# The entry of a gated-delta mixer on one core: unit order, gate rows and norm sums moved, one convolution placed in the delta rule

## The reference

```
qkv = silu(causal_depthwise_conv(h @ w_in[q, k, v], conv_w))        # 4 taps, 8 heads of 128
q, k = l2norm(q), l2norm(k)
beta = sigmoid(h @ w_in[b]);  g = -exp(a_log) * softplus(h @ w_in[a] + dt_bias)
o_a = gated_delta_rule_chunked(q, k, v, cumsum of g in chunks of 64, beta)
o_a = rmsnorm(o_a, dn_out_norm) * silu(h @ w_in[z])
o_b = stick_breaking_attention(rmsnorm(sb_q), rmsnorm(sb_k), sb_v)
x   = x + (sigmoid(ga) * (o_a @ w_branch_a) + sigmoid(gb) * (o_b @ w_branch_b)) @ w_out
```

## Time and profile before

| | us |
|---|---|
| median of 3 runs (lowest, highest) | 2456.24 (2454.42, 2457.91) |
| profiled execution | 2458.99 |
| its span, first to last instruction | 2457.2 |
| GpSimd busy | 1706.3 |
| VectorE busy, ScalarE busy | 1124.6, 1115.8 |
| first layer's mixer: unit 3 begins, last Gram product begins | 223.62, 266.74 |
| second layer's mixer: the same | 1056.27, 1099.40 |

### The profile page before, as it was taken

One profiled execution on the slowest core, in us unless ns is written; L12 is line 12 of the kernel. 1 busy time (PEld: TensorE's weight loads), 2 busy tenths in 40 slices (PEclk: granted clock), 3 DMA queues, 4 the chain that ended last, 5 costly groups with the idle time before them and its releaser, 6 DMA issues.

```text
span 2457.2 us, 40321 instructions
## 1 busy us (share of the span) xinstructions
PE 2352.2 (96%) x15688; PEld 2139.3 (87%) x15688; DVE 1124.6 (46%) x1945; ACT 1115.8 (45%) x1275; POOL 1706.3 (69%) x1340
## 2 busy tenths in 40 slices
PE   8999899999999999999999999999999999999997
PEld 7888889998988888888899889889888888888886
DVE  3335765422333333365554232333625665523766
ACT  4335344446443443454443544335555335555433
POOL 6998454554799899774455478997545997645995
PEclk9999999999999999999999999999999999999999
DMA  6555323323455555542333345565333555323553
GB/s 236 191 193 164 103 87 103 103 89 119 160 193 192 175 189 190 177 146 86 94 107 110 103 136 169 192 204 150 102 104 120 192 196 170 119 87 117 188 191 111
DMA packets 312197, 359.96 MB, mean 146 GB/s; under 512 B 18636, under 2 KB 291072, under 8 KB 311936
## 3 DMA queue, kind: packets, MB, share of 16 engines
q1 hardware_dynamic: 311866, 358.01, 44.8%
q10 hardware_dynamic: 198, 0.06, 0.0%
HBM read 357.00 MB, written 1.05 MB: 146 GB/s over the span
## 4 chain that ended last, share of the span: by engine, by line
PE 83%; DVE 10%; ACT 5%; issue 2%; POOL 1%; DMA 0%; ACTq 0%; DVEq 0%
PE ps L545 20%; PE ps L745 20%; PE ps L577 16%; PE ps L582 9%; PE ps L624 3%; PE ps L831 1%; PE ps L784 1%; PE ps L640 1%; PE ps L838 1%; PE ps L1116 1%; DVE sb_vT L1843 1%; DVE sb_kT L1843 1%; PE ps L840 1%; PE ps L611 1%; DVE sb_levels L1911 1%
## 5 line engine op out<-in xcount | busy, mean ns | idle before, releaser
L518 POOL TENSOR_TENSOR sb_lo<-sb_raw,sb_hi 128x512 fp32r<-128x512 f32 (+1 forms) x1336 | 1706.1, 1312 | 728.2 <-ACT sb_hi L1213 727.7
L1213 ACT ACTIVATE sb_hi<-sb_raw 128x2048 fp32r<-128x2048 f32 (+3 forms) x341 | 639.3, 1876 | 668.3 <-PE ps L582 349.2
L577 PE MATMUL ps<-sb_hT,sb_hi 128*128 128x512 f32 x1792 | 426.1, 390 | 0.0
L577 PEld LDWEIGHTS ps<-sb_hT,sb_hi 128*128 128x128 f32 x1792 | 332.7, 188 | 66.7
L745 PE MATMUL ps<-sb_hT,sb_hi 128*128 128x256 f32 x2304 | 312.4, 288 | 8.9 <-ACT sb_zT L1313 3.9
L745 PEld LDWEIGHTS ps<-sb_hT,sb_hi 128*128 128x128 f32 x2304 | 286.4, 191 | 15.3 <-ACT sb_zT L1313 4.3
L582 PEld LDWEIGHTS ps<-sb_hT,sb_lo 128*128 128x128 f32 x1792 | 229.8, 191 | 8.7
L582 PE MATMUL ps<-sb_hT,sb_lo 128*128 128x256 f32 x1792 | 232.4, 283 | 0.0
L1763 DVE TENSOR_TENSOR sb_yinv<-ps,sb_row 128x512 f32<-128x512 f32 x112 | 77.5, 692 | 334.9 <-PE ps L582 334.9
L545 PE MATMUL ps<-sb_hi,sb_o_h 128*128 128x512 f32 x560 | 219.5, 392 | 3.9 <-DVE sb_o_l L2219 3.0
L545 PE MATMUL ps<-sb_hi,sb_o_l 128*128 128x512 f32 x560 | 218.6, 390 | 0.0
(11 more groups left out here) (373 smaller groups left out, 3682.1 us busy)
## 6 DMA issues: line engine op xcount, KB each, us to landing
sb_raw<-in_ffn_w_in SPq DMA_DIRECT2D x88, 1024.0 KB, 5.1
sb_raw<-in_w_in SPq DMA_DIRECT2D x78, 1024.0 KB, 5.2
sb_raw<-in_ffn_w_out SPq DMA_DIRECT2D x44, 1024.0 KB, 4.9
sb_raw<-in_ffn_w_up SPq DMA_DIRECT2D x44, 1024.0 KB, 5.1
sb_raw<-in_ffn_w_down SPq DMA_DIRECT2D x22, 1024.0 KB, 4.8
sb_raw<-in_w_out SPq DMA_DIRECT2D x16, 1024.0 KB, 5.1
sb_raw<-in_w_branch_a SPq DMA_DIRECT2D x8, 1024.0 KB, 5.4
sb_raw<-in_w_branch_b SPq DMA_DIRECT2D x8, 1024.0 KB, 5.1
```

Source lines behind the costliest of these rows:

```text
L518: ins = nc.gpsimd.tensor_tensor(lo[:, slot, c], raw[:, slot, c], hi[:, slot, c].bitcast(F32), ALU.subtract)
L577: mm(ps[:, bank + i, :].rearrange("p (h n) -> p h n", h=2), wh[:, c, i * P:(i + 1) * P], hT_both[:, :, c, :], start=c == 0, stop=False, sk ...
L1213: fn(hi[:, slot, 0:width], raw[:, slot, 0:width], ACT.Copy).then_inc(hi_ready, 1)
```

## The change

Units 3 to 7 come in the order b, k, a, v, z. On TensorE the norm sums `pre(l, 0)` stand behind the second quarter of z, the small transposes of the gate rows between z and the last unit q1, and the 20 transposes are gone. ScalarE applies SiLU to q and k alone ahead of the squares (new helper `silus`) and to v and z behind the inverse roots; TensorE waits for the latter (`first_silu`) ahead of the transposes of k and v in the first delta rule. VectorE's gate rows use bank 7 instead of the bank of a, which is released as soon as a is read. VectorE no longer convolves q1 ahead of the first normalisation: it does so in two halves in the first delta rule, behind its first two steps, ahead of k1's halves. The plan and all later units are unchanged.

```diff
-FIRST = [("sv", 0), ("sv", 1), ("q", 0), ("z", 0), ("b", 0), ("k", 0), ("a", 0), ("v", 0), ("q", 1)]
+FIRST = [("sv", 0), ("sv", 1), ("q", 0), ("b", 0), ("k", 0), ("a", 0), ("v", 0), ("z", 0), ("q", 1)]
 B_AT, A_AT = FIRST.index(("b", 0)), FIRST.index(("a", 0))
...
         rows_act, rows_dve, rows_pe = sem("rows_act"), sem("rows_dve"), sem("rows_pe")
+        first_silu = sem("first_silu")
         pre_pe, pre_act, pre_dve = sem("pre_pe"), sem("pre_act"), sem("pre_dve")
...
                 wv("diff")
+                if c == 0:
+                    pe.wait_ge(first_silu, l + 1)
                 for p in range(4):
...
                 pe.wait_ge(start_loaded, 16)
-                for r in range(3, len(FIRST)):
+                for r in range(3, 7):
                     unit1(l, b, r)
+                for at, _ in enumerate(unit1_parts(l, b, 7)):
+                    if at == 1:
+                        pre(l, 0)
                 pe.wait_ge(rows_dve, ROWS_DVE.at(l, "beg"))
...
                 ins.then_inc(rows_pe, 1)
-                warm(2)
-                pre(l, 0)
+                unit1(l, b, 8)
                 with_units(chain(*(delta(l, c) for c in range(NPAIR))), DELTA_PLAN, lambda r: unit1_parts(l, b, r))
...
+            def silus(l, c, kinds):
+                for kind in kinds:
+                    freed(l, MIX1_ORDER.index((kind, c)))
+                for kind in kinds:
+                    buf = {"q": qT, "k": kT, "v": vT, "z": zT}[kind][:, 2 * c:2 * c + 2, :]
+                    ins = fn(buf, buf, ACT.Silu)
+                own.link(ins)
+                act.preload_act_table_set(LOGS)
             def pre_squares(l, half):
...
                 if half < NPAIR:
-                    for u in pair_units(c):
-                        freed(l, MIX1_ORDER.index(u))
-                    for buf in (qT, kT, vT, zT):
-                        ins = fn(buf[:, sl, :], buf[:, sl, :], ACT.Silu)
-                    own.link(ins)
-                    act.preload_act_table_set(LOGS)
+                    silus(l, c, ("q", "k") if half == 0 else ("q", "k", "v", "z"))
                 else:
...
                 mix_split(b, 5)
-                evac1(l, 3)
-                mix_split(b, 6)
                 act.wait_ge(unit_done, RING * b + (B_AT + RING + 1))
                 fn(beta_r[:, :], ps[0:HEADS, B_AT % 2, 0:S], ACT.Exp, scale=-1.0).then_inc(bank_free[B_AT % 2], 1)
+                mix_split(b, 6)
                 mix_split(b, 7)
-                mix_split(b, 8)
                 act.wait_ge(rows_dve, ROWS_DVE.at(l, "y"))
...
                 fn(e, e, ACT.Ln, bias=1.0).then_inc(rows_act, 1)
-                mix_split(b, 9)
+                pre_squares(l, 0)
+                mix_split(b, 8)
                 act.wait_ge(rows_dve, ROWS_DVE.at(l, "g"))
...
                 ins.then_inc(rows_act, 1)
-                mix_split(b, len(FIRST) + 1)
-                pre_squares(l, 0)
-                evac1(l, len(FIRST) - 1)
                 pre_roots(l, 0)
+                mix_split(b, 9)
+                evac1(l, 7)
+                silus(l, 0, ("v", "z"))
+                act.sem_inc(first_silu, 1)
+                mix_split(b, 10)
                 with_units(chain(*(delta(l, c) for c in range(NPAIR))), DELTA_PLAN, b, lambda r: evac1(l, r), mix_split)
...
-            def with_units(steps, todo, l, b):
-                late = []
+            def with_units(steps, todo, l, b, late=()):
+                late = list(late)
                 for at, _ in enumerate(steps):
...
                 y, e = sq[h8, 0, 0:S], sq[h8, 0, S:2 * S]
-                gates = ps[h8, A_AT % 2, S:2 * S]
+                gates = ps[h8, 7, S:2 * S]
                 dve.wait_ge(row_ready, 3 * l + 2)
...
                 evac1(l, b, 2)
-                evac1(l, b, 5)
+                evac1(l, b, 4)
                 dve.wait_ge(unit_done, RING * b + (A_AT + RING + 1))
                 ts(y, ps[h8, A_AT % 2, 0:S], hcol[:, 0:1], None, ALU.add).then_inc(rows_dve, 1)
+                dve.wait_ge(rows_dve, ROWS_DVE.at(l, "y"))
+                dve.sem_inc(bank_free[A_AT % 2], 1)
                 freed(l, B_AT)
...
                 own.link(V.tensor_tensor_scan(out=g_r[:, :], data0=cc("scan")[h8, :], data1=gates, initial=0.0, op0=ALU.mult, op1=ALU.add))
-                dve.sem_inc(bank_free[A_AT % 2], 1)
                 gc = g_r[:, :].rearrange("h (c n) -> h c n", n=CHUNK)
...
                    ALU.subtract).then_inc(rows_dve, 1)
+                evac1(l, b, 6)
                 dve.wait_ge(rows_act, ROWS_ACT.at(l, "eg"))
                 tt(y, beta_r[:, :], eg_r[:, :], ALU.mult).then_inc(rows_dve, 1)
-                evac1(l, b, 7)
                 dve.wait_ge(rows_act, ROWS_ACT.at(l, "high"))
...
                 dve.wait_ge(rows_dve, ROWS_DVE.at(l, "cols"))
-                evac1(l, b, 8)
                 pre_norm(l, 0)
-                with_units(chain(*(delta(l, c) for c in range(NPAIR))), DELTA_PLAN, l, b)
+                with_units(chain(*(delta(l, c) for c in range(NPAIR))), DELTA_PLAN, l, b, [(8, (0,)), (8, (1,))])
                 with_units(chain(*(stick(l, c) for c in range(NPAIR))), SB_PLAN, l, b)
```

## The result

The median of 20 runs is 2459.49 us (2454.95 to 2461.42), that of 20 runs of the kernel before on the same chip 2455.31 us (2450.64 to 2460.09): ratio 1.0013, 95% interval 1.0007 to 1.0019. The changed kernel is slower: by 3.2 us in the mean of its runs, by 4.2 in the median. The prediction had 2453.6 and "within 0.2%"; the time lies at the upper end of its range, on the other side of no change. The profiled execution took 2459.74 us (span 2458.0).

What follows compares the result with a forecast made beforehand. The prediction took TensorE, busy 96% of the span, as the bound. It summed 2 x 0.87 + 0.86 = 2.6 us, taking the profiled 2458.99 to 2456.4 and the median to 2453.6 us, range 2449.6 to 2459.8.

Steps and rivals of the forecast that it cites:

- Steps 1 to 3: First mixer's entry: warm-up and waits for squares and normalised k go, a wait ahead of k comes; 3.8 us saved.
- Steps 4 and 5: First delta rule: the moved convolution's second half adds 1.94 us, GpSimd slows the masks by 0.83 and 0.16.
- Step 6: TensorE waits at unit 10 for its bank until 272.3; 0.9 of 3.8 us left per layer, later trace unchanged.
- Step 8: TensorE's clock: one fall of 1.72 us on average, as before; half of the profiled run's fall goes, -0.86 us.
- the terms of the entry: Saving left behind the new wait at unit 10, 0.87 us per layer, counted for two layers.
- step 7: Added SiLU pair with table loads, rounding of unit 10, bank releases and changed load order: all put at nothing.
- Rival C: Clock falls at unit 10 and before the second level in both layers, four instead of one: 2459.6 us, chance 0.12.
- A: Delta rule takes in the moved convolution for nothing, all 3.8 us per layer stay: 2448.6 us, chance 0.10.
- B: As forecast, but GpSimd does not slow the masks and the clock does not fall: 2450.7 us, chance 0.14.
- D: Squares not ready after z's second quarter, so TensorE stops inside z: 2455.6 us, chance 0.06.

Runs made afterwards that it cites:

- sixth: Changed kernel with the 20 transposes per layer put back ahead of the wait at unit 10, and 62 idle ScalarE instructions per layer: 0.9987 of the kernel before.
- tenth: Changed kernel with 20 more idle TensorE semaphore instructions per layer: 1.0011 of the kernel before.
- fifth: Changed kernel with 39 TensorE and 62 ScalarE idle semaphore instructions more per layer: 1.0006 of the kernel before.
- first experiment: Changed kernel with 39 more idle TensorE semaphore instructions per layer: 1.0003 of the kernel before.
- twelfth: Changed kernel with the 20 transposes per layer ahead of the wait at unit 10, and 88 more idle TensorE instructions per layer: 0.9994 of the kernel before.
- eighth: Changed kernel, TensorE and ScalarE padded, four of six gate-row products ahead of unit 8's last two quarters, its convolution in one piece: 0.9972 of the kernel before.
- fourth: Kernel before without the 20 transposes ahead of the norm sums, nothing else changed: 1.0044 of the kernel before.
- eleventh: Changed kernel with 64 more idle TensorE semaphore instructions per layer: 1.0010 of the kernel before.

## Why the prediction was wrong, by its steps

- Steps 1 to 3 held: the squares' wait and the warm-up are gone, TensorE waits 0.89 us ahead of k and 0.82 ahead of v, and the quarter behind the Gram products and the transposes starts at 264.05 (264.0 forecast).
- Steps 4 and 5 held. L1906 starts at 262.40 (262.3), takes 1.46 (1.52), the second mask ends at 270.2 (270.4), the moved half at 272.1 (272.3).
- Step 6 held in its mechanism: the wait ends at 272.19. Its result, 0.9 us left per layer, appears only when the clock is kept: 279.67 in the sixth (279.8 forecast). In the changed kernel the second level starts at 280.73, where it was before.
- **Step 8 failed**, in the sentence "I count falls as likely as before, half a fall per layer". It put one fall of 1.72 us into the sum, and let half of it go. With the wait at unit 10 the clock fell in 12 of 12 layers of the six profiles that have it (TensorE idle for 2.96 us in one piece in eleven, for 0.57 and 2.02 in the tenth's first layer), and the falls cost 4.3 and 4.5 us by the means. The chance leaned on a stretch at 1.00 with 6.04 us of matmuls in 10, which holds waits of 2.08 and 1.88 us. In the first layer of the same trace the clock fell behind the same wait of 2.08 us:

```profile
581.34 0.70 PE L920 MATMUL ps<-sb_sq,sb_tok 128*128 128x256 f32 x2 [2.08 <-ACT sb_sq L1401]
```

```profile
580.00:590.00 10.00, 7.17 (x31) 6.35 (x32) 2.69 (x4) 7.68 (x9) 9.37 (x8) 0.66 0.31 99
```

  So that stretch was one of two that went opposite ways. Nor was the new wait like the old ones: from 15 us on no wait of the kernel before is longer than the 2.27 of the earlier trace rows, behind which the clock fell in one layer of two. Whether the length of the idle piece decides is argued from this, not shown. Without the falls at unit 10, the sixth gives -3.4 us (uncertain by 1.0), where the terms of the entry give 2 x 0.87 + 1.72 for the one fall of the kernel before.
- **The last sentence of step 6 failed**, "the trace runs on as before", and with it step 7, which lists what was put at nothing. The list had loads, roundings and semaphores, but not the program itself: 78 instructions fewer on TensorE moved the head of a loop that turns 1800 us later, and cost 2.2 to 2.3 us, up to 4.1.
- Rival C had the right place (the wait at unit 10) and the right sign, with four falls where there are two. That its 2459.6 is close to the measured 2459.5 is luck: without the cost of the code's place, which it did not have, the change stands at +0.9 us (fifth) to +1.2 (first), where C has +3.4. A and B needed unit 10 to start before 270; it started at 272.19. D never came: the squares end at 244.1, TensorE asks at 246.1.
- On the table load the trace still disagrees with the Trainium skill (ScalarE: Activation LUTs, What ACT_TABLE_LOAD costs): the added load runs from 252.56 for 1.28 us and the SiLU starts at 253.86, 0.02 us later, so the 1.38 us of drain are not to be seen.

The falls are not all of one length. From unit v's start behind the wait for k to the attention's wait of 2.08 us a layer takes 340.40 and 340.37 us in the sixth (341.20 and 340.43 in the twelfth). In the six profiles with the falls it takes 341.60 to 341.65 in seven layers and 342.56 to 344.06 in five. The mean is 1.7 us more, 3.4 for both layers, and so most of what the means show. In the longest, the first layer of the first experiment, the clock was 0.93, 0.50 and 0.72 in the three stretches of 4 us from 268.

Open: why 90 is a bad position and 130 is not, why the place costs 4.1 us with the eighth's entry and some 2 with the others, why the missing transposes of the fourth cost 8.5 us in the means, and why the tenth and eleventh (1.0011, 1.0010) are not as low as the first and fifth (1.0003, 1.0006); these intervals overlap.

## What to carry to other kernels

Filler ahead of a wait can be worth more than it takes: before taking it out, or before putting a wait of 2 to 4 us into a dense TensorE stretch, look at the granted clock behind every wait of about that length in the trace, and not at one stretch. When a local edit changes the number of an engine's instructions, compare the waits released by "issue" at every loop turn behind it, and pad with idle instructions to tell place from content. And where an engine is the chain, first fill its idle stretch: with the gate rows brought forward the eighth is 8.0 us below the fifth by the means, and 3.6 below the sixth, which keeps the clock too.

## What the runs showed of the hardware

- TensorE's wait at a loop's back edge depends on where the code stands: 2.35 to 3.02 us or nothing, by a shift of 40 to 80 instructions; 78 added semaphore instructions in the dense part themselves showed no cost (from unit v to the attention's wait the fifth takes 341.60 and 341.62 us in its two layers, the changed kernel 341.63 and 341.61).
- TensorE's granted clock fell behind 2.96 us of idle time 11 times out of 11, and once behind 0.57 and 2.02 us with 0.66 of work between; with 2.35 us of transposes ahead and 0.79 us idle, never in four. Behind 2.08 us of idle time it fell in one layer of the kernel before and not in the other. Behind 4.03 us it stayed low for 12 us.
